# Cached sequences: low parts of the probabilities on VectorE, and both blocks of value products one page earlier

## What is computed

```
def build_keys(c_kv, k_pe, w_uk, k_head_norm):
    k_nope = jnp.einsum('...lc,chd->...lhd', c_kv, w_uk)
    k_rope = jnp.broadcast_to(k_pe[..., None, :], k_nope.shape[:-1] + (QK_ROPE,))
    return rmsnorm(jnp.concatenate([k_nope, k_rope], axis=-1), k_head_norm)
s = jnp.einsum('qhd,khd->hqk', q, k) * SCALE
p = jax.nn.softmax(s, axis=-1)
o_lat = jnp.einsum('hqk,kc->qhc', p, c_kv)
return jnp.einsum('qhc,chd->qhd', o_lat, w_uv)
```

## Time and profile before

| | |
|---|---|
| median of 3 runs | 1552.35 us (1550.98 to 1555.8) |
| the profiled execution | 1550.25 us |
| its span | 1548.1 us |
| TensorE matmul busy | 1527.6 us, 99% |
| VectorE busy | 1036.4 us, 67% |
| ScalarE busy | 659.7 us, 43% |
| GpSimd busy | 663.6 us, 43% |
| mean granted TensorE clock | 0.997 |
| cached sequences | 721.2 to 1027.4 us |

### The profile page before, as it was taken

One profiled execution on the slowest core, in us unless ns is written; L12 is line 12 of the kernel. 1 busy time (PEld: TensorE's weight loads), 2 busy tenths in 40 slices (PEclk: granted clock), 3 DMA queues, 4 the chain that ended last, 5 costly groups with the idle time before them and its releaser, 6 DMA issues.

```text
span 1548.1 us, 32031 instructions
## 1 busy us (share of the span) xinstructions
PE 1527.6 (99%) x11182; PEld 1475.6 (95%) x11182; DVE 1036.4 (67%) x1672; ACT 659.7 (43%) x1258; POOL 663.6 (43%) x682
## 2 busy tenths in 40 slices
PE   8999999999999999999999999999999999999998
PEld 8999999999999999588999989988999999999998
DVE  4998888611269976865877777864669978784001
ACT  5453444522221242364666657662434444453110
POOL 3165455544445654320233333223552655564342
PEclk9999999999999999999999999999999999999999
DMA  6133333322333332002322222312222323342232
GB/s 174 42 105 99 87 103 98 95 77 75 82 85 99 85 110 61 1 1 55 84 64 61 63 62 62 88 55 76 85 77 71 103 81 101 89 128 58 76 86 70
DMA packets 231678, 122.82 MB, mean 79 GB/s; under 512 B 28415, under 2 KB 228327, under 8 KB 231572
## 3 DMA queue, kind: packets, MB, share of 16 engines
q1 hardware_dynamic: 230510, 120.83, 27.9%
q10 hardware_dynamic: 1070, 0.74, 0.2%
HBM read 118.31 MB, written 3.58 MB: 79 GB/s over the span
## 4 chain that ended last, share of the span: by engine, by line
PE 91%; DVE 4%; ACT 2%; issue 2%; DMA 1%; SPq 0%; DVEq 0%; ACTq 0%
PE ps L488 40%; PE ps L1546 27%; PE ps L1924 11%; PE ps L1816 1%; PE ps L1687 1%; PE ps L1741 1%; PE ps L1716 1%; PE ps L1855 1%; PE ps L1834 1%; PE ps L1884 1%; PE ps L1835 1%; DMA x_nat<-in_x_sample 1%; PE ps L1731 1%; PE ps L1693 1%; PE ps L1698 0%
## 5 line engine op out<-in xcount | busy, mean ns | idle before, releaser
L474 POOL TENSOR_TENSOR w_lobuf<-w_rawbuf,w_hibuf 128x256 fp32r<-128x256 f32 (+2 forms) x336 | 316.5, 973 | 369.3 <-ACT w_hibuf L467 369.3
L1546 PE MATMUL ps<-xs,w 128*128 128x288 f32 x3192 | 427.5, 296 | 2.2 <-DVE w L2050 2.2
L1546 PEld LDWEIGHTS ps<-xs,w 128*128 128x128 f32 x3192 | 426.8, 188 | 2.6 <-issue 2.6
L803 POOL TENSOR_TENSOR w<-w_raw,w 128x256 fp32r<-128x256 f32 x216 | 222.7, 1063 | 222.9 <-DVE w_raw L2038 142.9
L467 ACT ACTIVATE w_hibuf<-w_rawbuf 128x1024 fp32r<-128x1024 f32 (+1 forms) x90 | 104.8, 1165 | 359.7 <-PE ps L488 358.2
L488 PE MATMUL ps<-a_hi,w_hibuf 128*128 128x288 f32 x704 | 152.4, 297 | 0.0
L488 PE MATMUL ps<-a_hi,w_lobuf 128*128 128x288 f32 x704 | 152.2, 297 | 0.0
L488 PE MATMUL ps<-a_lo,w_hibuf 128*128 128x288 f32 x704 | 150.1, 294 | 0.0
L488 PE MATMUL ps<-x_hi,w_hibuf 128*128 128x288 f32 (+1 forms) x672 | 146.1, 299 | 1.7 <-DVE w_lobuf L2210 0.8
L488 PE MATMUL ps<-x_hi,w_lobuf 128*128 128x288 f32 (+1 forms) x672 | 144.7, 297 | 0.0
L488 PE MATMUL ps<-x_lo,w_hibuf 128*128 128x288 f32 (+1 forms) x672 | 144.5, 297 | 0.0
(11 more groups left out here) (352 smaller groups left out, 2757.2 us busy)
## 6 DMA issues: line engine op xcount, KB each, us to landing
w_raw<-in_ffn_w_gu SPq DMA_DIRECT2D x76, 256.0 KB, 2.9
up_rows<-in_ffn_w_gu SPq DMA_DIRECT2D x74, 256.0 KB, 3.2
c_nat<-in_cache_ckv SPq DMA_DIRECT2D x128, 128.0 KB, 2.0
w_rawbuf<-in_w_in SPq DMA_DIRECT2D x58, 256.0 KB, 3.1
w_rawbuf<-in_ffn_w_down SPq DMA_DIRECT2D x32, 384.0 KB, 4.0
w_rawbuf<-in_ffn_w_down SPq DMA_DIRECT2D x32, 320.0 KB, 3.4
w_rawbuf<-in_ffn_w_gu SPq DMA_DIRECT2D x24, 256.0 KB, 3.4
w_rawbuf<-in_w_out SPq DMA_DIRECT2D x16, 256.0 KB, 3.1
```

Source lines behind the costliest of these rows:

```text
L474: ins = pool.tensor_tensor(w_lobuf[:, r, part], w_rawbuf[:, r, part], w_hibuf[:, r % HIS, part].bitcast(F32), ALU.subtract)
L803: ins = pool.tensor_tensor(w7[b][:, slot, 1, part], w7_raw[b][:, slot, 1, part], w7[b][:, slot, 0, part].bitcast(F32), ALU.subtract)
L1546: mm = pe.matmul(ps[:, seven_bank(f, slot), 0:HALF], m, xs[:, slot, n, k, :], start=k == 0 and j == 0, stop=k == KH - 1 and j == 2)
```

## The change

VectorE makes the low parts of the probabilities in a sixth step of its softmax, at pp 5, behind `pages_lo` of the next pair and ahead of everything else of pp 5. POOL no longer does, so its splits follow each other. TensorE's two blocks stand ahead of pages 11 and 14 (before: 12 and 15). The first waits for VectorE's low part of the first half (count 5 of soft_step, which now has 8 counts a sequence), the second for the other half (count 6). ScalarE makes the high parts of pairs 4 to 7 after pages 10 and 11. The sum column, the fold, and VectorE's part of them move a page earlier too, and one tap moves from pp 5 to pp 7. No matmul is added or removed.

```diff
-        SOFT = 6
+        SOFT = 8
-        SPLITS = PAIRS + 2
+        SPLITS = PAIRS
-        LATE_AT = 11
+        LATE_AT = 10
         def pair_made(r, j):
-            return r * SPLITS + (EARLY_PAIRS + 1 if j < EARLY_PAIRS else j + 3)
+            return r * SPLITS + (j + 1)
...
             def squares(s, b, uses, prev, nxt):
                 if prev and stacked(s):
                     for j in range(EARLY_PAIRS):
                         split_pair(s - 1, 1 - b, j)
-                    for half in range(2):
-                        probabilities_low(s - 1, 1 - b, half)
                     for j in range(EARLY_PAIRS, PAIRS):
                         split_pair(s - 1, 1 - b, j)
...
                     for j in range(PAIRS):
                         pe.wait_ge(split_made, pair_made(r, j))
+                        if j in (0, PAIRS // 2):
+                            pe.wait_ge(soft_step, soft_steps(r) + (5 if j == 0 else 6))
...
-                            for _ in range({12: 4, 15: 4}.get(t, 0)):
+                            for _ in range({11: 4, 14: 4}.get(t, 0)):
                                 next(soft)
-                            if prev and k == 1 and t in ((7, 8, 15) if stacked(s) else (7, 8)):
+                            if prev and k == 1 and t in ((7, 8, 14) if stacked(s) else (7, 8)):
                                 next(soft)
-                        if prev and stacked(s) and t == NP - 1:
+                        if prev and stacked(s) and t == NP - 2:
                             next(soft)
...
                 if stacked(r + 1):
+                    for half in range(2):
+                        t = slice(half * NP // 2, (half + 1) * NP // 2)
+                        dve.wait_ge(p_done, exp_made(r, half))
+                        ins = dve.tensor_tensor(p_two[:, t, 1, :], s_buf[:, b, t, :], p_two[:, t, 0, :].bitcast(F32), ALU.subtract)
+                        if half:
+                            ins = dve.tensor_tensor(p_two[0:TS, NP, 1, :], s_buf[0:TS, b, NP, :], p_two[0:TS, NP, 0, :].bitcast(F32), ALU.subtract)
+                        ins.then_inc(soft_step, 1)
+                    yield
                     dve.wait_ge(lat_mm, r + 1)
...
-                    if prev and pp < (5 if stacked(s) else 6):
+                    if prev and pp < 6:
                         next(soft)
-                        for _ in range((0, 0, 0, 1, 1, 2, 2, 0)[pp]):
+                        for _ in range((0, 0, 0, 1, 1, 1, 2, 1)[pp]):
-                        if prev and stacked(s) and t == NP - 2:
+                        if prev and stacked(s) and t == NP - 3:
                             next(soft)
```

More of the change, by code:

```diff
@@ L518, in pair_made, with soft_steps @@
         def pair_made(r, j):
-            return r * SPLITS + (EARLY_PAIRS + 1 if j < EARLY_PAIRS else j + 3)
+            return r * SPLITS + (j + 1)
+        def soft_steps(r):
+            return r * SOFT if stacked(r + 1) else STACKED * SOFT + (r - STACKED) * 6
         def high_made(r, j):
@@ L909, in split_pair @@
                     .then_inc(split_made, 1)
[L911 to L918, removed]
             def squares(s, b, uses, prev, nxt):
@@ L1842, in soft_pe @@
                     yield
-                    pe.wait_ge(soft_step, r * SOFT + 5)
+                    pe.wait_ge(soft_step, soft_steps(r) + 7)
                     pe.matmul(ps[:, 7, 2 * P:2 * P + 1], fold[:, :, :].rearrange("p h n -> p (h n)"), o_lat[:, KL:KL + 1], start=True, stop=True)\
@@ L2579, in own @@
                     ins.then_inc(soft_step, 1)
-                    dve.wait_ge(soft_step, r * SOFT + k)
+                    dve.wait_ge(soft_step, soft_steps(r) + k)
                 dve.wait_ge(kpe_sq, r + 1)
@@ L2595, in soft_dve @@
                 yield
-                dve.wait_ge(soft_step, r * SOFT + 3)
+                dve.wait_ge(soft_step, soft_steps(r) + 3)
                 dve.wait_ge(new_copied, r + 1)
@@ L2612, in soft_dve @@
                     dve.wait_ge(p_summed, r + 1)
-                    own(dve.reciprocal(inv_den[:, :], ps[:, 7, 2 * P:2 * P + 1]), 6)
+                    own(dve.reciprocal(inv_den[:, :], ps[:, 7, 2 * P:2 * P + 1]), 8)
                     dve.tensor_scalar(fold_inv[:, :], fold[:, 0, :], inv_den[:, :], None, ALU.mult).then_inc(lat_scaled, 1)
```

## The result

The changed kernel takes 1579.98 us (median of 6 runs, 1576.33 to 1582.1), the kernel before 1551.83 (1550.67 to 1555.8). The ratio is 1.0179, with a 95% interval from 1.0164 to 1.0193: 28 us slower. The forecast was 1576, range 1567 to 1585.

The account below looks back on a forecast made before the run. TensorE, its matmuls filling 99% of the span, was taken as the bound. 1550.25 + 17.6 (first block's wait) + 5.6 (clock) = 1573.5; with 2.1 from profiled execution to median, 1575.6, rounded 1576 us, range 1567 to 1585.

Parts of the forecast that it names:

- The first block: Ahead of page 11, TensorE waits for VectorE's low part behind cT_lo of pair 6: 17.6 us net over six sequences.
- The clock: TensorE's clock falls to half behind four of the six new gaps, 1.4 us each: 5.6 us, bounds 0 and 9.
- rival 2: Every new TensorE gap brings a clock dip: 1579 us, or 1580 with low parts at 0.86 us; chance 0.22.
- The second block: Ahead of page 14: its inputs are ready at B + 7.4, TensorE comes about B + 8.1, so no wait.
- Sum column and fold: They keep their distance from the block; only in s = 6 up to 0.5 us, taken as 0.
- POOL, SP and the tap: POOL's lost work, SP's page loads and the tap moved to pp 7 change nothing in the time.
- Rival 3: Faster: low part ready when TensorE reaches the first block, 1.7 us of gaps won, 1550.7 us; chance 0.03.

Follow-up runs that it names:

- run 3: Changed kernel, but VectorE makes the first half's low part ahead of its sum of page 9, not behind cT_lo of pair 6: 1550.35 us.
- run 6: Changed kernel, but VectorE makes the first half's low part directly ahead of cT_lo of pair 6, not behind it: 1558.02 us.
- run 7: Changed kernel, but ScalarE makes the second half of the exponentials after page 10, so cT_hi of pair 6 comes ahead of it: 1566.36 us.
- run 5: Changed kernel plus 13 matmuls of ones on TensorE ahead of the first block's wait, ending before VectorE's low part: 1569.84 us.
- run 2: Kernel before the change with only the blocks, sum column, fold, high parts and tap a page earlier; low parts stay on GpSimd: 1554.93 us.
- run 4: Changed kernel plus 24 matmuls of ones on TensorE ahead of the first block's wait, which lasted longer than that wait: 1582.64 us.
- run 1: Changed kernel with only the low parts moved to VectorE; blocks, sum column, fold, high parts and taps at their old places: 1557.8 us.

## Why the prediction was right

*The first block.* The step that carried the sum held to a few hundredths: the new subtraction took 0.68 us (681 to 686 ns), the block started 3.3 us after TensorE's arrival in s = 1 to 5 (counted, as in the prediction, from where the square of page 9 lets it go on), and the gap ahead of page 12 went. By the list of waits the six sequences have 21.6 - 3.7 = 17.9 us more of them, against 17.6 net. Run 3 shows that the order alone makes the wait, runs 6 and 7 that each link of the chain (VectorE's cT_lo, ScalarE's exponentials) adds what its rows say, and run 5 leaves the waits without the clock: some 18 us.

*The clock.* The mechanism was right and the term too small: "I take four dips of six at 1.4 us: 5.6 us". The trace gives 27.3 - 17.9 = 9.4 us, run 5 about 10. The price of a stretch of 3.4 us was right (1.4 taken, 1.4 to 1.6 in the trace). The count was one too low, five in place of four, and the length failed: I took every half-clock stretch to be 3.4 us, as the one in the trace of before. Two were 6.83, at 2.5 each.

In both of the long ones the clock had fallen over a microsecond before TensorE got to work (782.38 against 783.50; 908.67 against 909.70). Where it had fallen 0.4 us before (867.71 against 868.10) the stretch stayed at 3.4. In the kernel before it had fallen 0.25 us before the next matmul (919.94 against 920.19), and no longer stretch followed. The same gap of the layer norm stands in every trace, and it bears this out: in runs 2, 6 and 7 the clock had fallen 1.2, 1.1 and 0.9 us before that matmul (run 6: 924.70 against 925.76), and there the stretch was 6.83; in the other traces that show one it fell later, and the stretch was 3.41. When it falls differs from place to place with the same gap, so the number of stretches and the long ones among them could not be foreseen from these rows.

This term accounts for most of the way from the forecast's 1576 to the measured 1580, inside the range. That rival 2 has 1579 to 1580 too is a coincidence: its premise, a dip behind every gap, is not what happened (s = 6 had none), and five dips, two of them long, cost what it had for six.

*The second block* did not wait, as worked out; it starts at 794.15 right behind its transposes. One sum there is off: 3.5, 2 and 2.3 make B + 7.8 and not 7.4. In run 5, where no half clock disturbs, GpSimd was done at B + 7.5 and TensorE came at B + 8.1. *Sum column and fold:* taken as 0 with up to 0.5 in s = 6; it was 0.3 in the trace (o_lat). *POOL, SP and the tap:* nothing, as said. Missed was s = 7: its page 2 waits 0.5 us for cT_lo in the changed kernel and in runs 2 to 7. There VectorE's second inverse of the layer norm (1.96 us) stands ahead of it. That TensorE comes sooner than before, because the fold no longer lies between, is read off the order and was not tried.

*Rival 3*, the faster end, named VectorE's pp 5 as the point that decides. Run 3 put the low part where the rival needed it, and the 28 us went. The 1.7 us of gaps that the rival hoped for did not come on top: run 3 has 1550.35 beside 1550.8 for the kernel before, which is no measurable gain. That the rival's figure was 1550.7 is chance; it was reckoned from 1552.35.

## What to carry to other kernels

Before a consumer is moved ahead, look up at which place in its producer's own order the input is made, and what stands ahead of it there; that the producer is idle in the mean says nothing (VectorE sat idle 1.3 us just ahead of the link that held it). Where work goes to a faster engine, compare when it starts and not how long it takes: GpSimd at 1.27 us was 2.5 us sooner than VectorE at 0.68. On TensorE, price an idle gap like these (2.3 us and more) at more than its length, and check that by filling it with harmless matmuls that end before the wait does.

## What the runs showed of the hardware

Idle time of TensorE and its clock, weight loads, six gaps of each of the first three sizes: behind 1.7 us (0.9 in s = 6, run 6) no half-clock stretch; behind 2.3 to 2.4 (1.5 in s = 6, run 7) four; behind 3.6 to 3.7 (2.8 in s = 6, changed kernel) five, two of these 6.83 us long. The layer norm's gap of 2.8 us in s = 5 stands once in each of the 11 traces: ten have a stretch behind it, three of these 6.83 us long, and run 5 has none. The clock fell between 1.2 us before TensorE was at work again and 1.5 us after. The Trainium skill (TensorE: Matmul & The Clock Gate, section "Why this matters for your kernels") advises against idle gaps of more than about 3 us between bursts of matmuls. The runs agree for the gaps of 3.6 us, where five of five fell to half clock; they differ below, where gaps of 2.3 to 2.8 us mostly fell too.

VectorE instructions with two SBUF inputs often took longer while GpSimd worked beside them. In s = 1 of the changed kernel the tap of 784.10 ran with GpSimd idle, the other two beside it:

```profile
784.10 0.74 DVE L2285 SCALAR_TENSOR_TENSOR y<-ext,cols,y 128x512 f32<-128x512 f32 x1
792.71 1.33 DVE L2285 SCALAR_TENSOR_TENSOR y<-ext,cols,y 128x512 f32<-128x512 f32 x1
794.22 1.27 DVE L2285 SCALAR_TENSOR_TENSOR y<-ext,cols,y 128x512 f32<-128x512 f32 x1 [0.18 <-DVE y L2285]
```

```profile
791.14 2.35 POOL L911 TENSOR_TENSOR c_lo<-c_nat,c_hi 128x512 fp32r<-128x512 f32 x2 [3.29 <-ACT c_hi L1305]
793.45 1.49 POOL L929 TENSOR_TENSOR ta<-kpe_nat 128x512 f32<-128x512 f32 x1
```

In run 1 the same taps took up to 1.78 us. That GpSimd is the cause was read off the traces and not tried by itself.
